# Down-projections of a two-block transformer step issued as pairs of 64-row matmuls on opposite PSUM banks

## The reference, cut to what matters

```python
def swiglu_ffn(x, wi, wo):                       # block 1, d_ff 2816, twice in each of 2 layers
    g, u = jnp.split(x @ wi, 2, axis=-1)
    return (jax.nn.silu(g) * u) @ wo             # down-projection: 2816 -> 1024
...
x = x + 0.5 * swiglu_ffn(rmsnorm(x, ffn1_norm[i]), ffn1_wi[i], ffn1_wo[i])
...
def squared_relu_mlp(h, w1, w2):                 # block 2, width 4096, once in each of 2 layers
    return jnp.square(jax.nn.relu(h @ w1)) @ w2  # down-projection: 4096 -> 1024
```

## Time and profile before

| | |
|---|---|
| median of three runs | 3396.18 us |
| profiled execution, its span | 3394.2 us |
| instructions in the profile | 43403, of them 15434 matmuls and 15434 weight loads |
| PE busy | 3374.7 us (99%) |
| weight loads (PEld) busy, beside PE | 2735.0 us (81%) |
| DVE, ACT, POOL busy | 49%, 31%, 45% |
| TensorE's granted clock | 9 tenths or more in all 40 slices |
| DMA | 92 GB/s in the mean |

### The profile page before, as it was taken

The page is one execution under the profiler, slowest core; times in us unless marked ns, Lnnn a source line. Parts: engine busy times, 40 slices in busy tenths (PEclk is TensorE's granted clock), DMA queues, the critical chain, the costliest instruction groups (busy, mean ns, idle before and its releaser), DMA issues.

```text
span 3394.2 us, 43403 instructions
## 1 busy us (share of the span) xinstructions
PE 3374.7 (99%) x15434; PEld 2735.0 (81%) x15434; DVE 1648.0 (49%) x1994; ACT 1052.8 (31%) x1414; POOL 1543.7 (45%) x1160
## 2 busy tenths in 40 slices
PE   9999999999999999999999999999999999999999
PEld 7888877788888888887678888887888888788887
DVE  5442236654423644223575442378580727857171
ACT  3222234332222322223433222236422123632122
POOL 4444443354444545443335444453354443335443
PEclk9999999999999999999999999999999999999999
DMA  4332322233333333333223333342233323223332
GB/s 152 98 99 93 112 76 68 75 99 99 97 101 92 100 96 96 99 106 81 69 75 96 96 99 99 93 103 55 66 96 99 96 97 75 61 70 108 95 99 81
DMA packets 496158, 311.26 MB, mean 92 GB/s; under 512 B 41792, under 2 KB 454827, under 8 KB 496043
## 3 DMA queue, kind: packets, MB, share of 16 engines
q1 hardware_dynamic: 494316, 307.21, 31.0%
q10 hardware_dynamic: 1727, 2.45, 0.2%
HBM read 305.94 MB, written 3.67 MB: 91 GB/s over the span
## 4 chain that ended last, share of the span: by engine, by line
PE 94%; DVE 4%; DVEq 1%; issue 1%; ACT 0%; ACTq 0%
PE bank L546 17%; PE bank L550 16%; PE bank L552 14%; PE bank L527 13%; PE bank L532 12%; PE bank L531 12%; PE bank L553 2%; PE mb L609 1%; DVE sd_p L2304 1%; PE bank L1155 1%; PE mb L1182 1%; PE mb L757 1%; DVEq L2089 1%; PE mb L861 0%; PE mb L901 0%
## 5 line engine op out<-in xcount | busy, mean ns | idle before, releaser
L502 POOL TENSOR_TENSOR wl<-raw,wh 128x512 fp32r<-128x512 f32 x1152 | 1542.6, 1361 | 1816.6 <-ACT wh L1332 1816.2
L1332 ACT ACTIVATE wh<-raw 128x1024 fp32r<-128x1024 f32 x576 | 608.6, 1057 | 1635.5 <-PE bank L527 840.8
L546 PE MATMUL bank<-xh,wh 128*128 128x512 f32 x2384 | 933.1, 391 | 0.0
L550 PE MATMUL bank<-xl,wh 128*128 128x512 f32 x2384 | 927.6, 389 | 0.0
L552 PE MATMUL bank<-xh,wl 128*128 128x512 f32 x2086 | 811.9, 389 | 0.0
L546 PEld LDWEIGHTS bank<-xh,wh 128*128 128x128 f32 x2384 | 447.4, 188 | 104.9 <-issue 11.8
L550 PEld LDWEIGHTS bank<-xl,wh 128*128 128x128 f32 x2384 | 447.6, 188 | 92.0 <-issue 0.5
L527 PE MATMUL bank<-hh,wh 128*128 128x512 f32 (+1 forms) x1216 | 472.5, 389 | 0.0
L532 PE MATMUL bank<-hh,wl 128*128 128x512 f32 (+1 forms) x1216 | 472.2, 388 | 0.0
L531 PE MATMUL bank<-hl,wh 128*128 128x512 f32 (+1 forms) x1216 | 472.2, 388 | 0.0
L552 PEld LDWEIGHTS bank<-xh,wl 128*128 128x128 f32 x2086 | 391.6, 188 | 82.1
(11 more groups left out here) (420 smaller groups left out, 3169.2 us busy)
## 6 DMA issues: line engine op xcount, KB each, us to landing
raw<-in_ffn_wi_dram SPq DMA_DIRECT2D x176, 512.0 KB, 3.7
raw<-in_mlp_w_dram SPq DMA_DIRECT2D x128, 512.0 KB, 3.7
raw<-in_w_in_dram SPq DMA_DIRECT2D x102, 512.0 KB, 3.6
raw<-in_ffn_wo_dram SPq DMA_DIRECT2D x88, 512.0 KB, 3.6
raw<-in_w_out_dram SPq DMA_DIRECT2D x32, 512.0 KB, 3.8
raw<-in_w_ple_gate_dram SPq DMA_DIRECT2D x16, 512.0 KB, 3.8
raw<-in_w_a_dram SPq DMA_DIRECT2D x8, 512.0 KB, 3.3
raw<-in_w_b_dram SPq DMA_DIRECT2D x8, 512.0 KB, 3.4
```

What stands on the lines that cost most here:

```text
L502: last = gp.tensor_tensor(wl[j][:, part], raw[j % RAW_SLOTS][:, part], wh[j][:, part].bitcast(F32), ALU.subtract)
L546: first = pe.matmul(out[0:width, :], h[:, c:c + width], rh[:, k, :], start=k == 0, stop=False)
L550: pe.matmul(out[0:width, :], h[:, c:c + width], rl[:, k, :], start=False, stop=False)
L1332: act.activation(wh[n % SPLIT_SLOTS][:], raw[n % RAW_SLOTS][:], ACT.Copy).then_inc(s.hi_ready, 1)
```

## The change

`down` and `three` are no longer used by the down-projections; a new helper `four_tiles` does one slab. It cuts each 128-row product in an upper (partitions 0 to 63) and a lower half (64 to 127), and issues them in turn, so that two 64-row matmuls that follow each other use different partitions and write to different banks. A slab has four slots: tiles (0, 1), (2, 3), (1, 0), (3, 2), the first of a slot's tiles taken by the upper rows, the second by the lower. A slot has 6 such pairs (2 k-tiles x 3 parts). A bank thus gets one row half in one slot and the other half two slots later. Before each slot (but the two that open the tiles) PE waits for its own semaphore `slot_done`, which the last matmul of a slot raises: the slot before the last one must be complete. In the last slab the third slot gives two tiles ready at once, and the fourth the other two. The FFN's loop on PE is written out. The semaphore `toep_row` gives up its place: its two waiters now wait for the second count of `setup_read`.

```diff
+            def four_tiles(B, L, n, t, k0, ah, al, first, last, inc=1):
+
+                h, l = wh[n % SPLIT_SLOTS], wl[n % SPLIT_SLOTS]
+                for slot, on in enumerate(((0, 1), (2, 3), (1, 0), (3, 2))):
+                    if first and slot < 2:
+                        for d in on:
+                            open_tile(B, L, t + d)
+                    else:
+                        pe.wait_ge(s.slot_done, slots[0] - (0 if last and slot == 3 else 1))
+                    for kk_ in range(2):
+                        for part in range(3):
+                            w, x = l if part == 2 else h, al if part == 1 else ah
+                            for rows, d in zip((UPPER, LOWER), on):
+                                c = kk_ * S + d * P
+                                done = pe.matmul(bank[(B.base_tile + t + d) % TILE_BANKS][:], w[rows, c:c + P], x[rows, k0 + kk_, :],
+                                                 start=first and slot < 2 and kk_ == 0 and part == 0,
+                                                 stop=last and slot >= 2 and kk_ == 1 and part == 2)
+                            if slot == 0 and kk_ == 0 and part == 0:
+                                done.then_inc(s.slab_used, 1)
+                    if last and slot >= 2:
+                        done.then_inc(s.tile_ready, 2 if slot == 2 else 1 + inc)
+                    else:
+                        done.then_inc(s.slot_done, 1)
+                        slots[0] += 1
...
-                    down(0)
-                    with pe.Fori(0, 2) as i:
-                        for q in range(1, 5):
-                            down(q, i)
-                    for q in range(9, FT // 2):
-                        down(q)
...
+                    for q in range(FT // 2):
+                        take_slab(Block1, L, n0 + q)
...
+                        four_tiles(Block1, L, n0 + q, t0, 2 * q, hh, hl, q == 0, q == FT // 2 - 1)
...
+                        def down(q):
+                            take_slab(B, L, n1 + q)
...
+                            four_tiles(B, L, n1 + q, t1, 2 * q, hh, hl, q == 0, q == 7, 2 if half and dh else 1)
...
-            dve.tensor_scalar(toep[:], bank[3][:, 0:TOEP], -1.0, None, ALU.mult).then_inc(s.toep_row, 1)
+            dve.tensor_scalar(toep[:], bank[3][:, 0:TOEP], -1.0, None, ALU.mult).then_inc(s.setup_read, 1)
```

More of the change, by code:

```diff
@@ L274, in program @@
         scratch = nc.dram_tensor("toeplitz_rows", [SW_H, P, TOEP], F32, kind="Internal").ap()
-        names = """split_done half_split slab_used hi_ready tile_ready tile_evacuated setup_first setup_const setup_rows setup_rel
-            setup_read setup_t setup_copied rel_psum toep_row toep_out toep_in consts_ready
+        names = """split_done half_split slab_used slot_done hi_ready tile_ready tile_evacuated setup_first setup_const setup_rows setup_rel
+            setup_read setup_t setup_copied rel_psum toep_out toep_in consts_ready
             x_final sq_ready ss_ready ss_psum inv_var rstd_ready xl_ready xa_ready
@@ L555, in unit @@
                 return last
+            UPPER, LOWER = slice(0, P // 2), slice(P // 2, P)
+            slots = [0]
+            def four_tiles(B, L, n, t, k0, ah, al, first, last, inc=1):
[21 more added lines that the diff above has]
+                        slots[0] += 1
             def xl_wait(B, L, k):
@@ L630, in _ @@
                 if j == KT - 1:
-                    pe.wait_ge(s.toep_row, 1)
+                    pe.wait_ge(s.setup_read, 2)
                 for t in range(NT):
@@ L651, in ffn @@
                     n0, t0 = n + 2 * FT + half * (FT // 2), t + 2 * FT + 4 * half
-                    def down(q, i=None):
-                        take_slab(Block1, L, n0 + q, i, 4)
-                        h, l = wh[(n0 + q) % SPLIT_SLOTS], wl[(n0 + q) % SPLIT_SLOTS]
+                    for q in range(FT // 2):
+                        take_slab(Block1, L, n0 + q)
                         if half == 0:
[L658 to L670, removed]
-                    down(0)
-                    with pe.Fori(0, 2) as i:
-                        for q in range(1, 5):
-                            down(q, i)
-                    for q in range(9, FT // 2):
-                        down(q)
+                            pe.wait_ge(s.hidden_ready, at(L, 2 * FT, wh_count + 2 * q + 2))
+                        four_tiles(Block1, L, n0 + q, t0, 2 * q, hh, hl, q == 0, q == FT // 2 - 1)
                         if k == 2 and half == 0 and q == 9:
@@ L1245, in _ @@
                         n1, t1 = n0 + HALF2 + 8 * dh, t0 + HALF2 + 4 * dh
-                        def down(q, i=None):
-                            take_slab(B, L, n1 + q, i, 4)
-                            h, l = wh[(n1 + q) % SPLIT_SLOTS], wl[(n1 + q) % SPLIT_SLOTS]
+                        def down(q):
+                            take_slab(B, L, n1 + q)
                             if dh == 0:
[L1251 to L1264, removed]
+                                pe.wait_ge(s.hidden_ready, at(L, FT2, 4 * FT + half * HALF2 + 2 * q + 2))
+                            four_tiles(B, L, n1 + q, t1, 2 * q, hh, hl, q == 0, q == 7, 2 if half and dh else 1)
                         if L and half and dh:
@@ L1375, in ffn @@
                 if L == 0 and k == 0:
-                    act.wait_ge(s.toep_row, 1)
+                    act.wait_ge(s.setup_read, 2)
                     act.dma_start(scratch.rearrange("h (r e) c -> (h r) e c", e=SW_H),
```

## The result

The changed kernel takes 3406.68 us (median of 9 runs, 3404.0 to 3407.15) beside 3396.84 us for the one before: ratio 1.0026, 95% interval 1.0016 to 1.0035. It is slower by about 9.8 us. The forecast was 3367.5 us, in a range of 3354 to 3390, with a chance of 0.18 for slower; the time that came is that of the rival "no gain per pair", 3406.

What follows compares the result with a forecast made beforehand. PE, busy 99% of the span, was taken as the bound; -38.7 (pairs) + 4.1 (entries and exits) + 4.4 (seams) + 1.5 (norm) = -28.7 us, from 3396.2 to 3367.5 us, range 3354 to 3390.

Steps and rivals of the forecast that it cites:

- no gain per pair: Rival: an fp32r pair costs 226.7 ns like a full-height matmul, leaving only overheads: 3406 us, chance 0.07.
- PE as the only bound: Whole kernel: PE is busy 99% of the span, so only PE's own work or new waits change the time.
- how many matmuls change: Down-projections of FFNs and MLP: 3552 full-height matmuls become 3552 pairs.
- What a pair costs: Down-projections: a pair takes 215.8 ns, 10.9 less than a full-height matmul, over 3552 pairs: -38.7 us.
- the control: Full-height plain float32 at L757: 16 passes in 4.51 us, taken as 15 ns each beyond their columns.
- L861's 2.5 ns: Plain float32 64-row pairs at L861: 215.8 ns a step, 2.5 ns beyond the columns, credited to half height.
- Entering and leaving: Switching PE to the 64-row form and back: 0.41 us a round trip, ten of them, +4.1 us.
- Seams: Where a second group reopens banks in FFNs and MLP halves: PE waits 0.55 us at each of 8, +4.4 us.
- The first wait: At each seam, the next group's first slot waits for DVE's adds and loads weights in the open: 0.45 us.
- The second slot's extra 0.1: At each seam, slot 1 waits for DVE's adds of tiles 2 and 3: another 0.1 us.
- The norm: Behind a second FFN, DVE's last add ends 0.77 us later and PE waits for it, twice: +1.5 us.
- Edits at nothing: The slot_done waits, instruction rate of the unrolled FFN, weight supply and swapped start-up semaphore cost nothing.

Runs made afterwards that it cites:

- f32_full: Kernel before, each down-projection product's three fp32r matmuls replaced by one full-height plain float32 matmul of the high parts: 3609.2 us.
- full_slots: Changed kernel with six full-height matmuls per slot instead of six 64-row pairs, waits, signals and unrolled code kept: 3400.6 us, ratio 1.0011 to the kernel before.
- late_ready: Kernel before, full height, only signals changed: last slab's tiles reported, and next group's opened, in twos: 3401.4 us, ratio 1.0011.

## Why the prediction was wrong

**PE as the only bound, and how many matmuls change**: right, 3552 more in the profile.

**What a pair costs**: wrong, and it alone decides the sign. The pair was priced at 215.8 ns and costs 226.7, so the term of -38.7 us is 0. Of the steps inside it, these held: that two fp32r streams and two loads share the array freely, and that the weights are loaded under the running pair. That members start within 0.01 us held for six pairs in ten, and the step doesn't depend on it. The step that failed is the control, "Same type, same loads, full height: 15 ns": it took a duration to the end of the last pass for a distance of starts, and f32_full measured 2.2 ns. Without it L861's 2.5 ns say nothing of height. The trace of before had three rows that would have shown it. One is L1064, read as "2 x 0.213 and the 0.2 that every group of another form pays": L861's group of the earlier trace rows takes 0.64 us for four steps of 0.11, so it pays 0.20 for the form; two 38-row fp32r matmuls in 0.66 us, less that 0.20, are 0.23 each, so the two steps have some 15 ns each left over beyond their columns. The other two are fp32r at another width and at the other clock. Kernel before, PE in order of time, the 256-column matmuls at its end:

```profile
3379.77 0.28 PE L532 MATMUL bank<-hh,wl 128*128 128x256 f32 x1
...
3380.97 0.28 PE L527 MATMUL mb<-hh,wh 128*128 128x256 f32 x1
```

The same kernel and view, 512 columns at the lower clock:

```profile
2941.66 0.63 PE L550 MATMUL bank<-cql,wh 128*128 128x512 f32 x1
...
2943.80 0.58 PE L546 MATMUL bank<-cqh,wh 128*128 128x512 f32 x1
```

And the busy times of that stretch, kernel before (its length, the sum and busy us and count of PE, PEld, DVE, ACT and POOL, the granted clock, the DMA share and GB/s):

```profile
2940.50:2944.00 3.50, 3.50 (x11) 2.35 (x8) 3.43 (x4) 2.99 (x2) 1.78 (x2) 0.54 0.10 30
```

With 256 columns 10 steps take 1.20 us, 120.0 ns for 106.7 of columns: 13.3 again, so it is a fixed amount per matmul. In the stretch whose granted clock is 0.54 in the mean (nearly all of it at 1.2 GHz), five steps of full-height fp32r take 2.14 us, 428 ns for 426.7 of columns: the 13.3 ns are gone. They show only where the array takes a column every 0.42 ns, and pairs change nothing about that.

**The rival "no gain per pair"** had the mechanism right, and its 3406 is the measured time. The number is partly luck: its seams (4.4) and norm (1.5) were too dear, its entries and exits (4.1) too cheap, and the ninth place was missing. I gave it 0.07. What it had for itself, that L861 runs at half rate, was the whole matter, and deserved more than one chance in fourteen: the pair's price had been seen only in a form that differed in the one respect that counts.

**Entering and leaving**: 4.1 forecast; 4.6 by full_slots against the changed kernel, 5.1 with the shorter wait at the norm set right, and 4.9 in the trace.

**Seams**: 4.4 forecast, 8 x 0.36 = 2.9 in the trace (3.4 with the longer steps behind them). The first wait came out at 0.28 + 0.08 instead of 0.45: DVE began 0.08 earlier than assumed, and its four adds took 2.65 us instead of 2.73. The second slot's extra 0.1 did not appear.

**The norm**: 1.5 forecast, 2 x 0.34 = 0.7 in the trace.

**Edits at nothing**: right, as far as the intervals reach. Waits and unrolling cost nothing that full_slots shows beside late_ready (3400.6 and 3401.4, each with its own before at 3396.9 and 3397.7), and PE's instructions came fast enough: 4 in 226.7 ns over whole FFN halves.

**The rule of the Trainium skill** that a weight load overlaps a running matmul only in another row group ("TensorE: Matmul & The Clock Gate", Part 3, The mechanism) is not borne out: two loads start at 299.74 beside the pair that started at 299.73 on the same rows. The same section also lets a load pass ahead when it goes to the background weight buffer; that case, which the prediction left out, would allow what the trace shows. The drain at a change of form, which "TensorEngine Tiling (Array Packing)", Key Properties, has, agrees with the about 0.5 us per round trip.

## What to carry to other kernels

Cut full-height matmuls into row tiles only when the contraction leaves rows empty: the second stream is free (226.4 ns a step alone, 226.7 as a pair), but a pair costs what one full matmul costs, and each round trip through the other form takes about 0.5 us. Before a comparison of two rows carries a forecast, take both from the same kind of reading (start to start), and look for a control with the same type and the same rate, not only the same shape. When tiles are reported in groups, the last group's lateness is paid wherever the next stage opens those banks at once; 3.7 us here came from signals alone.

## What the runs showed of the hardware

Beyond its columns a matmul with its weight load carries, at 2.4 GHz: 13.3 ns in fp32r at 512 and at 256 columns, at full height and as a pair; about 13 as a lone 64-row tile; 12.1 in bf16; 16.7 with 96 and 18.3 with 32 output columns; 2.2 to 2.4 in a plain float32 pass of two cycles a column; and about 1 in fp32r at 1.2 GHz. Going over to 64-row fp32r pairs costs 0.24 us and going back 0.25, the somewhat longer steps behind them included. It changes neither with height nor with the number of streams, and it doesn't shrink with the load. What it is was not settled: a kernel that keeps the weights between two matmuls would tell the load from the stream, and was not tried.
